# Two-layer hybrid diffusion backbone on one core: the order of work in the router of the mixture of experts

## What is computed

```
hx2 = modulate(rms_norm(x, g_norm2[l]), sh2, sc2)          # the rows that the experts read
s   = sigmoid(t @ w_router)                                # t: all tokens; 16 experts
sel = s + b_router
grp_score = sum(top_k(sel of each group of 4, 2))          # best group of 4 experts ...
_, eidx   = top_k(where(in best group, sel, -inf), 2)      # ... and its best two
wts = s[eidx] / sum(s[eidx])
for e in range(16):
    y   = (silu(t @ w_gate[e]) * (t @ w_up[e])) @ w_down[e]
    out = out + combine[:, e:e+1] * y
x = x + gt2 * out
```

## Time and profile before

| | |
|---|---|
| median of 3 runs | 1533.33 us (1530.64 to 1534.82) |
| the profiled execution: its time | 1535.0 us |
| its span, first to last instruction | 1533.2 us |
| mean granted clock of TensorE, share of full speed | 0.911 |
| PE busy | 1305.8 us (85% of the span) |
| DVE, ACT, POOL busy | 606.1, 411.2, 117.0 us |
| 16 DMA engines, mean rate | 249 GB/s, 381.25 MB moved |

### The profile page before, as it was taken

One profiled execution on the slowest core, in us unless ns is written; L12 is line 12 of the kernel. 1 busy time (PEld: TensorE's weight loads), 2 busy tenths in 40 slices (PEclk: granted clock), 3 DMA queues, 4 the chain that ended last, 5 costly groups with the idle time before them and its releaser, 6 DMA issues.

```text
span 1533.2 us, 19883 instructions
## 1 busy us (share of the span) xinstructions
PE 1305.8 (85%) x8082; PEld 819.7 (53%) x8082; DVE 606.1 (40%) x1069; ACT 411.2 (27%) x643; POOL 117.0 (8%) x111
## 2 busy tenths in 40 slices
PE   3889999899999799899989836998799858778873
PEld 1477777687777353234333335876688634222321
DVE  0445567676462621111121145557767351101112
ACT  1432236462341400010000026336556300000000
POOL 0000000000040020000000020009702010000001
PEclk9889999999999869899999957999999959979986
DMA  9676753222220599869997953763334469999995
GB/s 385 250 285 247 288 224 150 72 77 76 90 84 6 218 347 385 328 243 366 367 390 265 374 210 140 317 258 138 115 133 141 190 264 330 393 408 387 402 422 180
DMA packets 63951, 381.25 MB, mean 249 GB/s; under 512 B 9552, under 2 KB 14356, under 8 KB 24436
## 3 DMA queue, kind: packets, MB, share of 16 engines
q1 hardware_dynamic: 45056, 338.71, 56.6%
q10 hardware_dynamic: 14708, 24.36, 4.8%
q0 software_dynamic: 4096, 16.91, 3.1%
HBM read 358.71 MB, written 42.21 MB: 261 GB/s over the span
## 4 chain that ended last, share of the span: by engine, by line
issue 42%; PE 37%; DVE 8%; ACT 5%; DMA 5%; POOL 3%; ACTq 0%; POOLq 0%; DVEq 0%; SPq 0%
PE bank L1734 9%; PE bank L1735 8%; PE bank L1736 8%; PE bank L1742 2%; POOL m_lo L645 2%; DMA hrow_d<-in_hy_bias 1%; PE bank L1700 1%; ACT L679 1%; DMA raw<-in_mod 1%; DMA stage<-in_in 1%; POOL x_rows L659 1%; DMA yg<-y_rows,rowid 1%; PE bank L1999 1%; PE bank L1750 1%; DVE wlo L1099 1%
## 5 line engine op out<-in xcount | busy, mean ns | idle before, releaser
L2085 PE MATMUL bank<-wexp,xg 128*64 128x512 f32 (+1 forms) x1504 | 294.6, 646 | 60.0 <-DMA wexp<-in_expert 57.0
L1734 PE MATMUL bank<-h_hi,whi 128*128 128x512 f32 (+1 forms) x640 | 227.8, 356 | 6.8 <-DVE h_lo L1099 5.7
L1735 PE MATMUL bank<-h_lo,whi 128*128 128x512 f32 (+1 forms) x640 | 221.3, 346 | 0.0
L1736 PE MATMUL bank<-h_hi,wlo 128*128 128x512 f32 (+1 forms) x640 | 220.8, 345 | 0.0
L2085 PEld LDWEIGHTS bank<-wexp,xg 128*64 128x64 f32 (+1 forms) x1504 | 79.2, 131 | 237.1 <-issue 160.4
L1099 DVE TENSOR_TENSOR wlo<-stage,whi 128x2048 fp32r<-128x2048 f32 x56 | 132.0, 2365 | 66.2 <-ACT whi L679 53.5
L2100 PE MATMUL bank<-wexp,act_a 128*32 128x256 f32 (+1 forms) x1072 | 146.0, 497 | 6.8 <-DVE act_a L1099 6.5
L679 ACT ACTIVATE yrow<-bank 128x512 f32<-128x512 f32 (+1 forms) x47 | 23.8, 506 | 435.7 <-PE bank L2100 346.2
L1734 PEld LDWEIGHTS bank<-h_hi,whi 128*128 128x128 f32 x640 | 125.3, 196 | 27.8 <-DVE h_lo L1099 7.9
L1735 PEld LDWEIGHTS bank<-h_lo,whi 128*128 128x128 f32 x640 | 125.5, 196 | 13.4 <-issue 0.5
L1736 PEld LDWEIGHTS bank<-h_hi,wlo 128*128 128x128 f32 x640 | 125.3, 196 | 13.7
(11 more groups left out here) (282 smaller groups left out, 1703.0 us busy)
## 6 DMA issues: line engine op xcount, KB each, us to landing
wexp<-in_expert SPq DMA_DIRECT2D x192, 1024.0 KB, 16.3
stage<-in_in SPq DMA_DIRECT2D x40, 1024.0 KB, 4.9
stage<-in_mod SPq DMA_DIRECT2D x26, 1024.0 KB, 7.2
spare<-in_mod SPq DMA_DIRECT2D x14, 1024.0 KB, 18.3
x_rows<-in_c_zero SPq DMA_DIRECT2D x20, 512.0 KB, 7.3
y_rows<-in_c_zero SPq DMA_DIRECT2D x20, 512.0 KB, 8.8
stage<-in_out SPq DMA_DIRECT2D x8, 1024.0 KB, 4.8
raw<-in_mod SPq DMA_DIRECT2D x8, 1024.0 KB, 7.1
```

The lines of the kernel that those rows point to most:

```text
L1734: MM(o, w[0], x_[0], start=start, stop=False)
L1735: MM(o, w[0], x_[1], start=False, stop=False)
L1736: return MM(o, w[1], x_[0], start=False, stop=stop)
L2085: ins = MM(bank[0][g * w:(g + 1) * w, :], x_[:, 2 * j + k, :], wexp[:, z, j, c], start=(first_ == 0), stop=(last_ == 0))
```

## The change

Four things are done, in both layers alike where not said otherwise. PE makes all eight logit products first and all row transposes after them. ACT loads the table of the sigmoid before the blocks of `h2T`, not right before the sigmoid. Of the row copies, none is left ahead of the sigmoid on ACT nor ahead of the choice of experts on DVE: ACT takes banks 0 to 2`NT`-3 behind the sigmoid, and DVE the last two, behind `routed`. And all eight lead units (layer 0 only) stand behind the places. The waits are set to the new counts.

```diff
@@ gpsimd
-                pool.wait_ge(S("row_a"), T // P)
-                pool.wait_ge(S("row_d"), T // P)
+                pool.wait_ge(S("row_a"), 2 * (T // P) - 2)
+                pool.wait_ge(S("row_d"), 2)
@@ scalar
+                nc.scalar.preload_act_table(ACT.Sigmoid)
                 for k in range(KT):
                     act.wait_ge(S("hn"), (KT if l == 0 else 2 * KT) + k + 1)
                     for s in range(NS):
                         c = slice(s * SEQ, (s + 1) * SEQ)
                         fn(h2T[:, k, c], hn[:, k % 2, c], ACT.Identity, scale=amp[:, 1, k, s:s + 1],
                            bias=modT[:, 48 + 2 * k + s:49 + 2 * k + s]).then_inc(S("h2"), 1)
-                    if 4 <= k < 4 + NT and k % 2 == 0:
-                        rows_out_(k - 4)
 
                 act.wait_ge(S("lg"), 1)
                 fn(lgT[:, 0:T], bank[7][0:NE, 0:T], ACT.Copy).then_inc(S("lgT"), 1)
-                rows_out_(NT)
                 act.wait_ge(S("lg"), 2)
                 fn(rt[:, 0, 0:NT * NE], bank[7][:, 0:NT * NE], ACT.Sigmoid).then_inc(S("affin"), 1)
-                for b in range(NT + 2, 2 * NT, 2):
+                for b in range(2 * NT - 2):
                     rows_out_(b)
@@ vector
                     tt(hn[:, k % 2, 0:T], xT[:, k, 0:T], rs[:, 0:T], MUL).then_inc(S("hn"), 1)
-                for b in range(1, NT, 2):
-                    rows_out_(b)
...
                 ins.then_inc(S("routed"), 1)
-                for b in range(NT + 1, 2 * NT, 2):
+                for b in range(2 * NT - 2, 2 * NT):
                     rows_out_(b)
@@ tensor
                 for k in range(KT):
                     pe.wait_ge(S("h2"), NS * (k + 1))
                     ins = MM(bank[7][0:NE, 0:T], wr[:, k, :], h2T[:, k, 0:T], start=(k == 0), stop=(k == KT - 1))
-                    if k < 4:
-                        for t in range(NT):
-                            row = T_(row_bank(t)[:, k * P:(k + 1) * P], h2T[:, k, t * P:(t + 1) * P])
-                            if k == 3:
-                                row.then_inc(S("rows"), 1)
                 ins.then_inc(S("lg"), 1)
-                for t in range(NT):
-                    if NT + t >= 7:
-                        pe.wait_ge(S("row_a"), 1)
+                for b in range(2 * NT):
+                    if b >= 7:
+                        pe.wait_ge(S("row_a"), b - 6)
                     for k in range(4):
-                        row = T_(row_bank(NT + t)[:, k * P:(k + 1) * P], h2T[:, 4 + k, t * P:(t + 1) * P])
+                        row = T_(row_bank(b)[:, k * P:(k + 1) * P], h2T[:, 4 * (b // NT) + k, (b % NT) * P:(b % NT + 1) * P])
                     row.then_inc(S("rows"), 1)
-                    if t == 0:
+                    if b == 0:
                         pe.wait_ge(S("lgT"), 1)
...
-                if l < DEPTH - 1:
-                    pe.wait_ge(S("row_a"), 3)
-                    pe.wait_ge(S("row_d"), 2)
-                    lead_units(0, LEAD // 2)
                 pe.wait_ge(S("routed"), 1)
...
                 ins.then_inc(S("places"), 1)
                 if l < DEPTH - 1:
-                    lead_units(LEAD // 2, LEAD)
-                pe.wait_ge(S("row_a"), NT)
-                pe.wait_ge(S("row_d"), NT)
+                    pe.wait_ge(S("row_a"), LEAD_BANK + 1)
+                    lead_units(0, LEAD)
+                pe.wait_ge(S("row_a"), 2 * NT - 2)
+                pe.wait_ge(S("row_d"), 2)
```

## The result

| | before | after |
|---|---|---|
| median, us (lowest to highest, 6 runs each) | 1534.94 (1530.64 to 1540.98) | 1525.3 (1523.12 to 1526.93) |
| profiled execution / its span | 1535.0 / 1533.2 | 1524.2 / 1522.4 |
| mean granted clock | 0.911 | 0.913 |

The ratio is 0.9929, 95% interval 0.9913 to 0.9945.

A forecast was written before the change was run, and what follows sets the result against it. The prediction took the expert stages as partly bound by the weight stream, behind router chains held by PE's transposes and ACT's row copies. Layer 0's -5.5 and layer 1's -4.2 made -9.7 us, forecast 1524 on the median's scale, range 1518 to 1530.

The forecast's parts named there:

- PE starts picking: Layer 0, behind the lead units: PE begins picking 6.0 us later than before, at 547.6 in place of 541.52.
- sixth step: Layer 0's expert stage: PE ready at 617.4, finds its weights, products end at 621.7, 4.1 us sooner.
- layer 1, logits: Layer 1's router: logits end at 1221.9 in place of 1224.4, -2.5 us, bounds -3.6 and -1.1.
- layer 1 in all: Layer 1: logits -2.5 and `lgT` to sigmoid -1.7 make -4.2 us, moving the whole expert stage behind.
- Layer 0's logits: Layer 0's router: clock rises at 510.7 as before, `lgT` starts at 515.5 in place of 519.54, -4.0 us.
- Row copy and table load: Layer 0, `lgT` to sigmoid: 1.15 us in place of 2.50, -1.35, with the load inside ACT's earlier wait.
- Lead units: Layer 0, behind the places: all eight at the low clock take 21.8 us; places cost +0.3.
- What hides the lateness: Layer 0's expert stage: weight stream starts 5.05 us sooner and earlier weight waits absorb PE's lateness; -5.5 us taken.
- One sign named for being wrong: SP's queue, layer 0: held by the lead units, waiting longer for PE's last unit than for the rows.
- Rival 1: Layer 0: lead block eats the gain, only layer 1's 4.2 us stays, 1529 to 1531 us; 12%.
- rival 2: Layer 0: low clock outlasts the lead block through picking and first steps, slower, about 1538 us; 6%.
- Rival 3: Both routers: logits stay cold, -2.3 and -1.1 in place of -4.0 and -2.5, 1527 us; 12%.

The follow-up runs named there:

- e8: The changed kernel run again, with nothing altered: 1523.69 us, ratio 0.9921 to the kernel before.
- e5: The kernel before, with only the early load of the sigmoid's table added: 1532.48 us, ratio 0.999.
- e1: The changed kernel without the early table load, which stands right before the sigmoid again: 1525.08 us, ratio 0.9925 to the kernel before.
- e3: The changed kernel with the row transposes of blocks 0 to 3 put back between the logit products: 1529.98 us, ratio 0.9956 to the kernel before.
- e4: The kernel before, with only the lead units' move made, all eight behind the places: 1535.88 us, ratio 0.9995.
- e6: The changed kernel with every product of the lead units made twice: 1531.86 us, ratio 0.9975 to the kernel before.
- e9: The changed kernel with filler matmuls, results never read, in layer 1 alone: 1523.01 us, ratio 0.9928 to the kernel before.
- e11: The changed kernel with 20 unread filler matmuls between layer 0's lead units and the picking: 1540.58 us, ratio 1.0041 to the kernel before.
- e7: The changed kernel with unread filler matmuls in idle PE time of both layers: 1520.05 us, ratio 0.9896 to the kernel before.
- e2: The changed kernel with four lead units ahead of the wait for `routed` again, four behind the places: 1526.87 us, ratio 0.9948 to the kernel before.

## Why the prediction was right

The forecast was 1524.0, in 1518 to 1530; measured 1525.3, and -10.8 us between the profiled executions where the sum said -9.7. By its own steps, times counted from each layer's first `h2T`:

| step | predicted | measured |
|---|---|---|
| layer 0, `lgT` behind the first `h2T` | 10.2 | 10.36 (e8 10.00) |
| `lgT` to sigmoid, layer 0 and 1 | 1.15 and 0.8 | 1.10 and 0.81 |
| layer 0, `ex` and the loads of rows | -5.05 | -4.90 and -4.83 |
| PE starts picking | 6.0 later | 6.5 later |
| PE's weight waits, 540 to 630 us | nearly gone | none |
| sixth step: PE ready, gate and up products end | 112.2, 116.5 | 112.1, 115.7 |
| layer 0 in all | -5.5 | -6.9 at the seventh step, -6.7 at the end of the layer |
| layer 1, logits | -2.5 | -1.6 (e8 -2.6) |
| layer 1 up to `ex` | -4.2 | -3.3 (e8 -4.3) |
| layer 1 in all | -4.2 | -6.6 (e8 -4.4) |

*Layer 0's logits.* The assumption that the clock rises at the same instant as before was right: low until 5.4 us behind the first `h2T` before and 5.5 now (4.7 in e8).

*Row copy and table load.* The 1.35 us were right as a sum (1.40 measured). The load is all of it if it is taken out first (1.4, e5); if the copy goes first, that is worth 0.6 and the load 0.8 (e1).

*Lead units.* Priced at 21.8 us cold; 22.1 measured, up to the start of the picking. The price was right, but the clock that it rests on isn't a property of the order: in e1, which differs only in where the table is loaded, the same eight units had full clock from 532 us on, and so they did from about 25 to 28 us behind the first `h2T` in e3, e4 and e6; they ran cold in all four runs whose layer 0 up to the last unit is the changed kernel's (after, e8, e9, e11). That they were cold as forecast was in part luck.

*What hides the lateness.* Right, down to the instant at which PE is ready for the sixth step. The size taken was too small, -5.5 against -6.9, in two terms. The step's products ended 4.9 us sooner (120.6 before, 115.7 now) and not 4.1, since they took 3.64 us where four times 1.07 was allowed. And the clock behind the step stayed high, which was worth 2.0 us (5.2 from there to the seventh step in place of 7.2) where 1.4 were taken. One sign named for being wrong came true by its letter: SP waited longer for PE's last unit (15.2 us) than for the rows behind it (8.2). That sign doesn't tell what it was meant to, since the two waits follow one another; the unit was over 8.2 us before the rows were back, so it held nothing, as the forecast said. Both ways of going wrong are now measured: earlier than the weights, PE loses its clock (e1, e6, e7), and with a first product later than about +60 at full clock (121 less the 60.45 of e11) every further microsecond is lost (e11). The changed kernel stands on the crossing by chance: PE's path and the stream's, in e7 and e2, all end at 121. e9, with the same layer 0 and a first product at +59.4, is already at +121.9.

*Layer 1.* The forecast's own terms for the logits (one block at 0.42, four at 0.84, three at 0.42) end at 1221.6 and not at 1221.9, which would make it -2.8. In the profiled run the clock stayed low through the logits (1212.00 to 1217.50 at 0.50, 6.34 us for the sixteen), which is between the forecast and its bound, and cost 1 us; e1, e2 and e8 have `lgT` at 6.08, the forecast's figure. Behind `ex` the layer gained 3.3 us more than it was given in the profiled run, and 0.1 in e8, with 25 and 27 waits for weights where before there were 28. I can't attribute those 3 us; the two executions of the changed kernel themselves differ by some 2 us in this layer.

*The mixer.* A term that the sum didn't have: over all runs, with not an instruction of it changed, layer 1's mixer took 321.2 to 325.5 us. A profiled span therefore can't confirm a gain below some 4 us; the medians do. It also made the sum look better than it was: the two router terms came to -13.2 together (-11.5 in e8) where -9.7 was forecast, and 2.5 us that have nothing to do with the change stand against them in the profiled pair. That the total is so close is in part luck.

*Rivals.* Rival 1 (the lead block eats the gain) and rival 2 (the cold clock outlasts it) both had their first half come true, PE 6.5 us late at half clock; the margin at the sixth step, as computed, decided. e11 has rival 2's lateness, brought about by more work and not by the clock. Rival 3 came true in part, in layer 1 (-1.6). Of the change's parts, the order of logits and transposes is worth some 4 to 5 us of the 10 (e3 against the changed kernel), the lead units' move nothing (e4, e2), and the early load nothing that can be measured by itself (e1, e5). What is left, some 5 us, would be the row copies' move, which no run has alone: that is by subtraction and not shown.

## What to carry to other kernels

Where a stage has two feeders, find the instant at which both meet, and count time only on the later one: engine time saved on the earlier one turns into a wait, and a wait on TensorE can take its clock as well (e1, e2, e6, e7). A block of work that is "only" moved should be priced at both clock levels, against that instant. Take small changes at one place from markers relative to the stage's own start, and the whole from medians.

## What was not expected of the hardware

- With weights landing at +114.3 and +114.0, the seventh step began at +123.6 where PE had waited (e1) and at +120.9 where it hadn't. But in e2, where PE came early as well, the last piece landed at +112.8, and its seventh step began at +121.1: in the end neither won.
- Being busy by the record did not bring the clock up: from 525.0 to 569.5 PE was busy for 43.54 of 44.50 us at 0.50. In e1 the same units, with the first 4 us of them as cold, had 1.00 from 532.2 to 559.0 with PE busy for 22.51 of 26.80 us. In e6, with twice the products, they ran at full clock from 532.6 at the latest.
- After a row copy between `lgT` and the sigmoid, and without one, the sigmoid came 1.10 us behind `lgT` (e5, after): `lgT` itself (0.59) and ACT's wait for the four transposes on PE (0.51) fill it.
